# Another order of the SBUF tables: the split weights start 40 instead of 48 bytes behind a multiple of 64

## What is computed

```
first:   x += 0.5*swiglu(rmsnorm(x));  x += hgrn2_mixer(rmsnorm(x));  x += 0.5*swiglu(rmsnorm(x));  x += sigmoid(h@Wg)*(p@Wp)
         shared keys and values from x
         x += 0.5*swiglu(...);  x += mla_mixer(...);  x += 0.5*swiglu(...);  x += sigmoid(h@Wg)*(p@Wp);  x = rmsnorm(x)
second:  x += even_mixer(rmsnorm(x));  x += conv_ffn(rmsnorm(x));  x += odd_mixer(rmsnorm(x));  x += conv_ffn(rmsnorm(x))
swiglu(h) = (silu(h @ W_in[:, :2816]) * (h @ W_in[:, 2816:])) @ W_out
conv_ffn(h) = the same, with a causal convolution of width 3 on h @ W_up ahead of the gate
```

## Time and profile before

| | |
|---|---|
| median of three runs | 1819.7 us (1817.01, 1819.7, 1828.51) |
| the profiled execution | 1823.98 us, of which 1822.1 us are its span from the first to the last instruction |
| PE busy | 1750.2 us (96%), 14492 matmuls |
| DVE, ACT, POOL busy | 65%, 53%, 19% |
| mean granted TensorE clock | 0.99 |
| read from HBM | 296 MB, 163 GB/s over the span |

### The profile page before, as it was taken

One profiled execution on the slowest core, in us unless ns is written; L12 is line 12 of the kernel. 1 busy time (PEld: TensorE's weight loads), 2 busy tenths in 40 slices (PEclk: granted clock), 3 DMA queues, 4 the chain that ended last, 5 costly groups with the idle time before them and its releaser, 6 DMA issues.

```text
span 1822.1 us, 36683 instructions
## 1 busy us (share of the span) xinstructions
PE 1750.2 (96%) x14492; PEld 1714.1 (94%) x14492; DVE 1190.6 (65%) x1764; ACT 957.6 (53%) x1097; POOL 351.6 (19%) x280
## 2 busy tenths in 40 slices
PE   7999899989999899999999999999899999989998
PEld 7999899979999899998998999988799999989998
DVE  6665688976565666556456555665477766567776
ACT  5444667764444754444345444565455455655553
POOL 2000500020004600036663000566400020020001
PEclk9999999999999999999999999999999999999999
DMA  5656323335555445544444555434245443345552
GB/s 218 225 190 242 128 101 115 99 119 208 198 190 185 156 176 193 188 141 135 137 138 154 187 187 185 170 128 151 93 170 199 177 180 139 117 162 185 185 206 92
DMA packets 45168, 298.25 MB, mean 164 GB/s; under 512 B 5024, under 2 KB 5408, under 8 KB 15920
## 3 DMA queue, kind: packets, MB, share of 16 engines
q1 hardware_dynamic: 45104, 297.38, 46.1%
HBM read 296.31 MB, written 1.05 MB: 163 GB/s over the span
## 4 chain that ended last, share of the span: by engine, by line
PE 80%; DVE 10%; ACT 5%; issue 3%; DMA 1%; POOL 0%; SPq 0%; ACTq 0%; DVEq 0%
PE wk L379 15%; PE wk L380 15%; PE wk L381 15%; PE acc L379 8%; PE acc L380 8%; PE acc L381 8%; DVE sumsq L678 2%; DVE x_lo L457 1%; PE wk L1033 1%; PE wk L391 1%; PE wk L390 1%; PE wk L389 1%; DVE x L422 1%; ACT w_hi L325 1%; ACT tmp L619 1%
## 5 line engine op out<-in xcount | busy, mean ns | idle before, releaser
L325 ACT ACTIVATE w_hi<-raw 128x2048 fp32r<-128x2048 f32 (+5 forms) x300 | 533.3, 1788 | 405.8 <-PE wk L381 333.8
L380 PE MATMUL wk<-x_lo,w_hi 128*128 128x256 f32 x2560 | 715.9, 280 | 0.0
L379 PE MATMUL wk<-x_hi,w_hi 128*128 128x256 f32 x2208 | 624.7, 283 | 19.0 <-DVE x_lo L457 13.3
L2603 POOL TENSOR_TENSOR w_lo<-raw,w_hi 128x512 fp32r<-128x512 f32 (+1 forms) x274 | 350.8, 1316 | 1455.7 <-ACT w_hi L325 1455.7
L381 PE MATMUL wk<-x_hi,w_lo 128*128 128x256 f32 x2208 | 618.0, 280 | 0.0
L351 DVE TENSOR_TENSOR w_lo<-raw,w_hi 128x2048 fp32r<-128x2048 f32 (+2 forms) x218 | 483.9, 2221 | 171.5 <-ACT w_hi L325 171.5
L380 PEld LDWEIGHTS wk<-x_lo,w_hi 128*128 128x128 f32 x2560 | 483.5, 189 | 0.4
L379 PEld LDWEIGHTS wk<-x_hi,w_hi 128*128 128x128 f32 x2208 | 421.4, 191 | 25.2 <-DVE x_lo L457 15.4
L381 PEld LDWEIGHTS wk<-x_hi,w_lo 128*128 128x128 f32 x2208 | 416.8, 189 | 0.0
L379 PE MATMUL acc<-h_hi,w_hi 128*128 128x256 f32 x1376 | 389.5, 283 | 16.3 <-DVE h_lo L2192 4.8
L381 PE MATMUL acc<-h_hi,w_lo 128*128 128x256 f32 x1376 | 385.9, 280 | 0.0
(11 more groups left out here) (323 smaller groups left out, 2138.4 us busy)
## 6 DMA issues: line engine op xcount, KB each, us to landing
raw<-w_ffn_loop SPq DMA_DIRECT2D x120, 1024.0 KB, 4.8
raw<-w_conv_loop SPq DMA_DIRECT2D x60, 1024.0 KB, 4.8
raw<-w_mla_loop SPq DMA_DIRECT2D x18, 768.0 KB, 4.3
raw<-w_hgrn_loop SPq DMA_DIRECT2D x10, 896.0 KB, 4.6
raw<-w_ple_gate SPq DMA_DIRECT2D x8, 1024.0 KB, 4.7
raw<-w_odd_loop SPq DMA_DIRECT2D x10, 768.0 KB, 4.2
raw<-w_even_loop SPq DMA_DIRECT2D x6, 1024.0 KB, 4.8
raw<-w_odd_proj SPq DMA_DIRECT2D x6, 1024.0 KB, 4.8
```

The source lines that it names most:

```text
L325: nc.scalar.activation(w_hi[slot][:, 0:n], raw[slot][:, 0:n], ACT.Copy).then_inc(S("hi_ready"), 1)
L379: nc.tensor.matmul(dst, hi, a_hi, start=start, stop=False, skip_group_check=True)
L380: nc.tensor.matmul(dst, hi, a_lo, start=False, stop=False, skip_group_check=True)
L2603: last = nc.gpsimd.tensor_tensor(w_lo[slot][:, a:b], raw[slot][:, a:b], w_hi[slot][:, a:b].bitcast(F32), ALU.subtract)
```

## The change

Three lines that take SBUF tensors move: `eps` (4 bytes a partition) to in front of the weights' parts, `par` (1996 bytes) to behind them. No instruction, wait, transfer or loop is added, removed or moved; only the addresses in them are others.

```diff
         x_lo_2 = sb("x_lo_2", [P, KD, SEQ], F32R)
-        par = sb("par", [P, N_PARAMS])
         cst = sb("cst", [P, N_CONSTS])
         rstd = sb("rstd", [P, SEQ])
         rstd_tok = sb("rstd_tok", [P, 2 * TB])
         sumsq = sb("sumsq", [P, SEQ])
         ln_ms = sb("ln_ms", [P, SEQ])
         ln_tok = sb("ln_tok", [P, 2 * TB])
+        eps = sb("eps", [P, 1])
         w_hi = [sb(f"w_hi{s}", [P, SLOT_TILES * P], F32R) for s in range(SLOTS)]
         w_lo = [sb(f"w_lo{s}", [P, SLOT_TILES * P], F32R) for s in range(SLOTS)]
+        par = sb("par", [P, N_PARAMS])
         tmp = sb("tmp", [P, 8, SEQ])
         zero = sb("zero", [P, 512], F32R)
-        eps = sb("eps", [P, 1])
```

## The result

The changed kernel takes 1854.14 us (median of four, 1846.81 to 1856.93), the kernel before 1822.47 (median of four, 1817.01 to 1828.51). The ratio on record is 1.0155, with a 95% interval of 1.0112 to 1.0199: slower by 1.55%, clear of the noise, and above the range that was given. The profiled execution took 1846.81 us, 22.8 more than the one of before, and is the shortest of its four.

A forecast was written before the change was run, and what follows sets the result against it. The prediction took PE's pace through its weight-load and matmul pairs to bound the kernel. Its terms for weights, ScalarE and VectorE work, and transfers summed 0 + 0 + 0 onto the 1819.7 us median, rounded to 1820, range 1792 to 1843.

The forecast's parts named there:

- What bounds the kernel, and what hangs on the pace: Whole kernel: PE busy 96% of the span; all matmuls at the shorter pace 29.4 us less, at the longer 29.1 more.
- The two paces: Six feed-forward loops: three at about 113.1 ns a matmul, three at about 117.6, 4.45 ns apart; one loop changing is 6.4 us.
- The start of the weights: Nearly every weight load: start moves from 48 to 40; direct cost 0, with ends -29.4 and +29.1 us.
- the nearest rows: Narrow matmuls at 111.8 ns, score matmuls with both operands in `work` at 111.9: 0.1 ns for an odd start, 1.4 us.
- the earlier trace: Not a name in the prediction; the descriptions fit its score-matmul row (operands in `work`), then its narrow-matmul row.
- The fourth rival: Allocation: padding to some boundary keeps the weights from moving as tabled; time as before, chance within no change's 0.52.
- The second rival: PE's pace: at 40 the streams of reads always meet, all stretches at 117.6 ns; 29.1 us slower, 1849 us, chance 0.16.
- The first rival: PE's pace: at 40 all or nearly all stretches run at 113.1 ns; 1795 us, or 1790 from the median, chance 0.26.
- third: Rival on every weight load: longer by one part in 32, 3.5 ns a pair; 46 us slower, 1866 us, chance 0.06.
- The rule of lines of 16 bytes: Skill's rule on SBUF reads: each new line costs; a weight tile at 48 fills 32 lines, at 40 touches 33.
- Outside the loops: 4,587 wide matmuls outside the feed-forward loops, half of them taken to be at the longer pace.
- The transfers, ScalarE and VectorE: Transfers, weight rounding and subtraction, norms: cost 0, with 0 to 3 us as bounds for all that isn't PE's pace.

The follow-up runs named there:

- w40_alone: The kernel before with pads of 14 columns ahead of the weights and 2 behind, `par`, `cst` and the norm's tiles left in place: 1856.90 us.
- w0: The kernel before with pads of 4 and 12 columns ahead of and behind the weights; the four runs of this program had medians of 1847.98 to 1853.19 us.
- w8: The kernel before with pads of 6 and 10 columns around the weights, really the same program as w0; the four medians are 1847.98 to 1853.19 us.
- w56: The kernel before with pads of 2 and 14 columns around the weights, really the same program as w0; the four medians are 1847.98 to 1853.19 us.
- w52: The kernel before with pads of 1 and 15 columns around the weights, really the same program as w0; the four medians are 1847.98 to 1853.19 us.
- a16_w0: The kernel before with pads of 4 and 12 columns around both the split activations and the weights, real distance 160: 1877.00 us, the longest.
- d64_after: The changed kernel with 448 bytes of padding ahead of the weights, making their distance to the activations 64 again: 1824.03 us, ratio 1.0033.

## Why the prediction was wrong

It priced rightly what hangs on PE's pace, and then put the change's own hold on that pace at nothing: no change was forecast, and 1.55% more was measured. Point by point:

- **What bounds the kernel, and what hangs on the pace.** Right. PE's pace is all that an address is seen to have moved. The two paces, the 6.4 us for a loop and the 29 us for the whole are borne out: 19.3 us between two kernels whose profiled executions differ by three loops.
- **The start of the weights: cost 0, "by the nearest rows".** This is the step that failed. The nearest rows, and the earlier trace rows, weren't near. In the earlier trace rows both operands lie in one tensor, `work`, so the change doesn't move one against the other at all. In the earlier trace rows it does, and these narrow pairs kept 111.7 ns in the changed kernel, while the wide pairs of the same code (`token_tile`) went from 117.1 to 118.8 on the mean and those of the loops to 118.7. So what the earlier trace rows lacks is 256 columns that move; that these are read while the next weight tile is loaded, and that the two reads get in each other's way, is an inference. Measured for the step: +5.3 ns on the matmuls at the short pace and +0.9 on the others, 26.6 us in the loops, where the sum had 0.
- **Where the tensors start.** Also wrong, and ahead of the step: 48 and 40 behind a multiple of 64 were sums of sizes. The fourth rival was half right, since the allocation does pad; but it doesn't pad the move away. I had given this a sentence and the chance of no change. To ask for the place of a tensor would have shown a move from 64 to 128.
- **The second rival, slower.** It came nearest, with a chance of 0.16: it had all stretches at one long pace, 1849 us, and one long pace is what came. That "the streams always meet" isn't shown, and what counts isn't the start in 64 bytes, which it named. It took the longest pace to be the 117.6 ns of before; by first to last start that is 117.8, and the pace that came was 118.7. The range's end of 1843 left this rival out on purpose, and that is why the time lies above it.
- **The first rival** fell with its sign, and the **third** too: it had 3.5 ns more on every pair, and the two kinds of loops grew by 5.3 and by 0.9. The narrow pairs, with which I argued against it, say nothing of it, since the weights aren't the loaded operand there; nor do the score matmuls, since `work` in truth starts at a multiple of 32. The rule of lines of 16 bytes, weighed there, has no bearing on the change, because both kernels start every weight tile at a multiple of 32.
- **Outside the loops.** I had 4,587 matmuls at stake, half of them at the longer pace, and that was right: the mean step there was 115.6 ns before, halfway between 113.3 and 117.8, and 118.8 in its place cost 12 us. What the sum didn't have is that waits and clock move the same stretches: they came out 3.7 us shorter in this execution and 5.9 longer in w40_alone's. PE's waits were the shorter in both (103.5 and 107.1 us for 113.4); why isn't shown.
- **The transfers, ScalarE and VectorE** show no cost, as predicted: 1909 and 2289 ns, and at the start the wait for x.

I took the spread of the before runs as a sign that a stretch's pace isn't fixed by the addresses alone. That holds: one program, run as w0, w8, w56 and w52, had its loops at other paces each time. But I drew too much from it. The addresses fix which paces there are to choose from. What picks one at a loop's entry, and why a distance of 64 or 320 allows 113.3 ns, wasn't shown; I have no run that looks inside the reads.

## What to carry to other kernels

Where PE runs pairs of weight load and matmul without a gap, its pace can hang on where the stationary operand lies against the moving one, modulo a few hundred bytes. A table that moves by some bytes was worth up to 3.5% of this kernel (a16_w0), and any change that adds or reorders tensors in between can bring this along unasked. So compare the pace in a gapless window before explaining a small difference otherwise, take the addresses from the allocation and not from sums of sizes, and pin the distance with a pad once a good one is found.

A row is only near to a case if it has the same two things going on at once, and if the change would move them against each other as it does in the case. The same operand at an odd start isn't enough.

## What the runs showed of the hardware that I had not expected

- A weight load of 128 float32r columns with a matmul of 256 comes every 113.3, 117.3, 117.8, 118.3, 118.7 or 120.0 ns at a granted clock of 1.00, sharp values that last for 1,300 to 1,500 pairs. Which of them occur goes with the operands' distance modulo 512 (one shift by 512 was tried; a period of 256 isn't ruled out): 120.0 at 0 and 160, 118.3 at 32, 113.3 or 117.8 at 64 and 320, 117.3, 118.7 and once 120.0 at 96, 118.7 at 128, 117.8 at 192, 113.3 once and else 117.8 at 448.
- The Trainium skill (SBUF — State Buffer, "Who interferes with whom") gives PE two read ports, one for the moving operand and one for weight loads, and calls them "independent". In speed they aren't, by these runs: moving one operand against the other by 64 bytes costs 5.3 ns a pair. The same section says that PE never waits on anyone, which is said of other engines; no run here tests it.
- One and the same kernel is spread over 23 us (the kernel before, 1808.68 to 1831.85 in thirteen runs on one chip), where all wide matmuls' choice of pace is worth 29 us. That this choice is the cause, and how much of it the granted clock is instead, is an inference from executions that were profiled once each. Both do move: d64_after has two short loops more than the kernel before and is only 6.3 us shorter in its profiled execution, with a clock of 0.986 for 0.990.
